# Attention in a two-layer fp32 backbone: probabilities turned by plain transposes, values multiplied four query blocks at a time, inverse sums applied to the result

## What is computed

```python
s_win = jnp.einsum("bqjhd,bqrjchd->bhqjrc", qb, kw) + bias[None]
s_ctx = jnp.einsum("bqjhd,bnhd->bhqjn", qb, k_ctx)
logits = jnp.concatenate([s_win.reshape(...), s_ctx], axis=-1)
p = jax.nn.softmax(logits.astype(jnp.float32), axis=-1)
out = (jnp.einsum("bhqjrc,bqrjchd->bqjhd", p_win, vw)
       + jnp.einsum("bhqjn,bnhd->bqjhd", p_ctx, v_ctx))
```

## Time and profile before

| what | value |
|---|---|
| median of three runs | 2733.43 us (2731.22 to 2735.35) |
| span of the profiled execution, first to last instruction | 2731.1 us |
| time of that execution beside its span | not listed; the span is 2.3 us under the median |
| PE busy | 2582.5 us (95%), 12026 instructions |
| PE weight loads busy | 2108.8 us (77%) |
| DVE busy | 1236.3 us (45%) |
| POOL busy | 1070.7 us (39%) |
| ACT busy | 583.4 us (21%) |
| attention: first logits to first matmul of the output projection | 417.06 to 730.16 us |

### The profile page before, as it was taken

The page is one execution under the profiler, slowest core; times in us unless marked ns, Lnnn a source line. Parts: engine busy times, 40 slices in busy tenths (PEclk is TensorE's granted clock), DMA queues, the critical chain, the costliest instruction groups (busy, mean ns, idle before and its releaser), DMA issues.

```text
span 2731.1 us, 33304 instructions
## 1 busy us (share of the span) xinstructions
PE 2582.5 (95%) x12026; PEld 2108.8 (77%) x12026; DVE 1236.3 (45%) x1748; ACT 583.4 (21%) x1070; POOL 1070.7 (39%) x529
## 2 busy tenths in 40 slices
PE   7898897989998999999999989999899999999999
PEld 3677776878886888888888868888678888888887
DVE  5666647867457433333222363433752222222224
ACT  4533334545323000000000140000320001000002
POOL 2223337654366333333433313343434444333330
PEclk9999998999999999999999999999899999999999
DMA  8333344321223333331111101111111111111111
GB/s 284 113 118 116 108 137 105 74 43 48 81 82 117 107 108 108 108 108 62 46 47 53 47 16 47 47 54 47 39 47 47 46 47 53 46 54 46 46 31 62
DMA packets 213972, 204.15 MB, mean 75 GB/s; under 512 B 31371, under 2 KB 184694, under 8 KB 213366
## 3 DMA queue, kind: packets, MB, share of 16 engines
q1 hardware_dynamic: 207398, 184.05, 22.6%
q10 hardware_dynamic: 5904, 16.78, 1.6%
q0 software_dynamic: 576, 2.10, 0.2%
HBM read 185.07 MB, written 19.81 MB: 75 GB/s over the span
## 4 chain that ended last, share of the span: by engine, by line
PE 77%; DVE 11%; issue 6%; ACT 3%; DMA 2%; POOL 1%; DVEq 0%; SPq 0%; ACTq 0%; POOLq 0%
PE bank L652 23%; PE bank L653 23%; PE bank L654 23%; PE bank L825 3%; PE bank L770 2%; DMA mod_in_p<-in_mod_w 1%; DVE h L1275 1%; DVE x_conv L1395 1%; PE bank L733 1%; DVE sumsq L1233 1%; DVE pt_lo L1477 1%; PE bank L815 1%; DVE scaled L1253 1%; PE bank L816 1%; DVE lru_i L1411 1%
## 5 line engine op out<-in xcount | busy, mean ns | idle before, releaser
L525 POOL TENSOR_TENSOR w_hi<-raw,ones 128x1024 fp32r<-128x1024 f32 x200 | 392.0, 1960 | 1360.3 <-PE bank L654 1115.2
L652 PE MATMUL bank<-act_hi,w_hi 128*128 128x512 f32 x2176 | 855.3, 393 | 15.3 <-DVE act_lo L1259 8.6
L653 PE MATMUL bank<-act_hi,w_lo 128*128 128x512 f32 x2176 | 851.6, 391 | 0.0
L654 PE MATMUL bank<-act_lo,w_hi 128*128 128x512 f32 x2176 | 851.0, 391 | 0.0
L528 POOL TENSOR_TENSOR w_lo<-raw,w_hi 128x1024 fp32r<-128x1024 f32 x200 | 508.9, 2544 | 15.7
L652 PEld LDWEIGHTS bank<-act_hi,w_hi 128*128 128x128 f32 x2176 | 411.4, 189 | 107.4 <-DVE act_lo L1259 11.5
L654 PEld LDWEIGHTS bank<-act_lo,w_hi 128*128 128x128 f32 x2176 | 411.3, 189 | 86.3
L653 PEld LDWEIGHTS bank<-act_hi,w_lo 128*128 128x128 f32 x2176 | 411.5, 189 | 85.0
L1275 DVE SCALAR_TENSOR_TENSOR h<-bank,mods,h 128x512 f32<-128x512 f32 x432 | 320.6, 748 | 246.6 <-PE bank L654 244.4
L1511 DVE TENSOR_TENSOR hid_f<-silu_g,bank 128x512 f32<-128x512 f32 x88 | 60.6, 688 | 707.4 <-PE bank L654 706.1
L652 PE MATMUL bank<-hid_hi,w_hi 128*128 128x512 f32 x704 | 280.7, 399 | 15.2 <-DVE h L1275 15.1
(11 more groups left out here) (183 smaller groups left out, 2713.6 us busy)
## 6 DMA issues: line engine op xcount, KB each, us to landing
raw<-in_ffn_w_gu SPq DMA_DIRECT2D x88, 512.0 KB, 3.8
mod_in_f<-in_mod_w SPq DMA_DIRECT2D x48, 512.0 KB, 4.6
raw<-in_ffn_w_down SPq DMA_DIRECT2D x44, 512.0 KB, 3.5
mod_in_p<-in_mod_w SPq DMA_DIRECT2D x32, 512.0 KB, 4.3
raw<-in_o_w_in SPq DMA_DIRECT2D x24, 512.0 KB, 3.8
raw<-in_e_w_in SPq DMA_DIRECT2D x20, 512.0 KB, 5.4
mod_ring<-in_mod_w SPq DMA_DIRECT2D x16, 512.0 KB, 4.5
raw<-in_e_w_out SPq DMA_DIRECT2D x16, 512.0 KB, 4.2
```

Of the source, the lines that this page charges most:

```text
L525: nc.gpsimd.tensor_tensor(w_hi, raw[:, parity, :], ones[:, 0:1].to_broadcast([P, UNIT]), ALU.mult).then_inc(s_hi, 1)
L652: pe.matmul(dst, w_hi, x_hi, start=first, stop=False)
L653: pe.matmul(dst, w_lo, x_hi, start=False, stop=False)
L654: return pe.matmul(dst, w_hi, x_lo, start=False, stop=last)
```

## The change

The probabilities stay as the exponentials are, without a division. A step's context logits are copied into `probs` next to the window's by a DVE operation of the same kind as the window's, which yields their minimum; one ACT instruction then takes all exponentials with one sum. Wide steps take 640 window columns (five full tiles) in place of 576. PE turns the tiles with plain transposes against the identity. Values are multiplied for four steps at once, each value tile by all the steps that read it, 128 to 512 columns, all rows; the products of a block are dealt over three of the following four steps (three spans each, the last has two). For a block, DVE takes four reciprocals in one instruction, PE spreads them over the partitions by four matmuls against the identity, ACT copies the spread rows to SBUF, and DVE multiplies the result with them into `y_f`; ACT and DVE split that.

The order changes with it: PE turns step j, then spreads or multiplies values of the block before, then scores step j+3. The loop of two rounds is written out. Most buffers of the stage move: two heads' raw keys and queries go to buffers of their own, the recurrent results are all reloaded at once and split by POOL after all heads, and the first three output weights are split once the block before the last is multiplied. The output projection begins with the recurrent half of its inputs and waits for the attention half only then. h is reloaded once all scores are done.

```diff
@@ PE @@
-                pe.wait_ge(s_exp, STEPS * i + s + 1)
+                if s >= 2:
+                    pe.wait_ge(s_min, s - 1)
...
-                    return pe.matmul(dst, probs[s % 4][:, src], inv_diag[:, s % 4, :], start=True, stop=True)
...
+            def turn_probs(s):
+
+                p, w, of = probs[s % 3], width(s), slots(s % TT)
+                pe.wait_ge(s_exp, s + 1)
+                if s:
+                    pe.wait_ge(s_ptl, 2 * s - 1)
+                for n in range(4):
+                    mm = pe.transpose(bank[:, 4, n * P:(n + 1) * P], p[:, of[n] * P:(of[n] + 1) * P], ident[:])
...
+                if 4 in of:
+                    pe.transpose(bank[:, 5, 0:P], p[:, of[4] * P:(of[4] + 1) * P], ident[:])
+                for x in range(CT):
+                    mm = pe.transpose(bank[:, 5, (x + 1) * P:(x + 2) * P], p[:, w + x * P:w + (x + 1) * P], ident[:])
...
+            def inverse_spread(g):
+
+                pe.wait_ge(s_inv, g + 1)
+                if g:
+                    pe.wait_ge(s_invr, g)
+                for j in range(4):
+                    mm = pe.matmul(bank[:, 7, j * P:(j + 1) * P], inv[:, 4 * g + j:4 * g + j + 1].to_broadcast([P, P]), ident[:],
+                                   start=True, stop=True)
...
+            def values(g, part):
+
+
+                slot, buf, every = g // 4 % 2, g % 2, spans(g % 2)
+                if part == 0:
+                    pe.wait_ge(s_ptl, 8 * g + 8)
...
+                    if g:
+                        pe.wait_ge(s_yf, g)
+                for n in range(3 * part, min(3 * part + 3, len(every))):
+                    to, tile, i0, i1 = every[n]
+                    mm = product(bank[:, 6, i0 * P:i1 * P], (v_hi[:, slot, tile, :], v_lo[:, slot, tile, :]),
+                                 pt_hi[buf][:, i0:i1, to, :], pt_lo[buf][:, i0:i1, to, :], n == 0, n == len(every) - 1)
...
+            for j in range(-3, STEPS + 4):
+                if 0 <= j < STEPS:
+                    turn_probs(j)
+                if j >= 4 and j % 4 == 0:
+                    inverse_spread(j // 4 - 1)
+                if j >= 5 and j % 4:
+                    values((j - 5) // 4, (j - 5) % 4)
+                if j + 3 < STEPS:
+                    scores(j + 3)
@@ ACT @@
+                nc.scalar.activation(probs[s % 3][:, 0:w], probs[s % 3][:, 0:w], ACT.Exp, bias=low_all[:, s:s + 1], scale=-1.0,
+                                     accum_out=sums[:, s:s + 1]).then_inc(s_exp, 1)
...
+                nc.scalar.copy(inv_rows[rows, :], bank[rows, 7, :]).then_inc(s_invr, 1)
...
+                nc.scalar.copy(act_hi[block_of(g)], y_f[block_of(g)]).then_inc(s_yh, 1)
@@ DVE @@
+                steps.run(V.tensor_tensor_reduce(out=probs[s % 3][:, w:w + CTX], in0=bank_f[:, o + w:o + w + CTX],
+                                                 in1=zero[:, 0:1].to_broadcast([P, CTX]), scale=1.0, scalar=FAR, op0=ALU.add,
+                                                 op1=ALU.min, accum_out=low_ctx[:, s:s + 1]))
+                V.tensor_tensor_reduce(out=probs[s % 3][:, 0:w], in0=bank_f[:, o:o + w], in1=bias_t[:, hd % 2, at0:at0 + w],
+                                       scale=1.0, scalar=low_ctx[:, s:s + 1], op0=ALU.add, op1=ALU.min,
+                                       accum_out=low_all[:, s:s + 1]).then_inc(s_min, 1)
...
+            def inverse_sums(g):
+                dve.wait_ge(s_exp, 4 * g + 4)
+                V.reciprocal(inv[:, 4 * g:4 * g + 4], sums[:, 4 * g:4 * g + 4]).then_inc(s_inv, 1)
...
+            def y_scaled(g):
+                rows, pair, sl = block_of(g)
+                dve.wait_ge(s_pv, g + 1)
+                dve.wait_ge(s_invr, g + 1)
+                V.tensor_tensor(y_f[rows, pair, sl], bank[rows, 6, :], inv_rows[rows, :], ALU.mult).then_inc(s_yf, 1)
...
+            for j in range(-2, STEPS + 7):
+                if j + 2 < STEPS:
+                    logits(j + 2)
+                if j >= 8 and j % 4 == 0:
+                    y_scaled(j // 4 - 2)
+                if 0 <= j < STEPS:
+                    turned_low(j)
+                if j >= 3 and j % 4 == 3 and j < STEPS:
+                    inverse_sums(j // 4)
+                if j >= 10 and j % 4 == 2:
+                    y_low(j // 4 - 2)
@@ POOL @@
+                steps.run(nc.gpsimd.tensor_copy(mid[:, 0:9, :], edge[:, 2:11, :]))
+                steps.run(nc.gpsimd.memset(mid[:, 9, :], FAR))
...
+            pool.wait_ge(s_rin, 16 * LT)
+            for j in range(LT):
+                split_lru(j)
+            for j in range(2 * FT):
+                free = (s_pv, BLOCKS - 1) if j < 3 else (s_yf, BLOCKS) if j == 3 else used_o(j - 4)
+                split(U_O + j, j % 4, j % 2, free)
@@ SP @@
+            for j in range(LT):
+                sp.dma_start(r_f[:, j, :], r_spill[j]).then_inc(s_rin, 16)
...
+            sp.wait_ge(s_sc, STEPS)
             sp.dma_start(h[:, 0:3, :], h_spill[:, 0:3, :]).then_inc(s_reload[0], 16)
```

More of the change, by code:

```diff
@@ L286, in backbone, with slots, spans, block_of @@
         V_ORDER = list(range(TT, V_TILES)) + list(range(TT))
[L287 to L294, removed]
+        STEPS = TT * HEADS
+        BLOCKS = STEPS // 4
+        LABELS = 6
+        def slots(b):
+            first, count = window(b)[0] // P, 4 + window(b)[1]
+            labels = [c if b < 4 else TT - 1 - c for c in range(first, first + count)]
+            return {0 if n == LABELS - 1 else n: r for r, n in enumerate(labels)}
+        def spans(half):
+            out_ = []
+            for n in (1, 2, 3, 0, 4, 5):
+                c = n if half == 0 else TT - 1 - n
+                at_ = [i for i in range(4) for f, wide in (window(4 * half + i),) if f // P <= c < f // P + 4 + wide]
+                out_.append((0 if n == LABELS - 1 else n, c, at_[0], at_[-1] + 1))
+            return out_[:3] + [(5 + x, TT + x, 0, 4) for x in range(CT)] + out_[3:]
+        def block_of(g):
+            hd, half = divmod(g, 2)
+            return slice(64 * (hd % 2), 64 * (hd % 2) + 64), hd // 2, slice(half * HALF, (half + 1) * HALF)
+        def width(s):
+            return MID if window(s % TT)[1] else HALF
         GROUPS = ((0, 0), (1, 0), (0, 1), (1, 1), (0, 2), (2, 0), (2, 1), (2, 2), (3, 0), (3, 1))
@@ L582, in split_head @@
                 slot = head % 2
+                k_from, q_from = (k_raw0, q_raw0) if head < 2 else (k_raw, q_raw)
                 pool.wait_ge(s_hraw, 64 * (head + 1))
@@ L799, in _, with scores @@
             pe.wait_ge(s_vev, V_TILES)
-            def scores(i, s):
+            def scores(s):
                 hd, b = divmod(s, TT)
@@ L879, in project_out @@
                 pe.wait_ge(s_split, U_O + half * FT + m + 1)
-                return columns(dst, (m + 2) % 4, act_hi, act_lo, slice(half * HALF, (half + 1) * HALF))
+                w_hi, w_lo = w_slot(slot)
+                sl = slice(half * HALF, (half + 1) * HALF)
+                for n in range(FT):
+                    k = (n + LT) % FT
+                    if half * FT + m == 0 and k == 0:
+                        pe.wait_ge(s_yl, BLOCKS)
+                    w = (w_hi[:, k * P:(k + 1) * P], w_lo[:, k * P:(k + 1) * P])
+                    mm = product(dst, w, act_hi[:, k, sl], act_lo[:, k, sl], n == 0, n == FT - 1)
@@ L882, in _ @@
+                return mm
             out_groups(0, project_out, N_F0)
@@ L1489, in _ @@
[L1489 to L1500 removed]
+                    dve.wait_ge(s_bias, hd + 1)
```

282 lines of the change are left out of this document (101 added, 181 removed).

## The result

The changed kernel takes 2635.82 us at the median of four runs (2631.84 to 2639.73) where the kernel before takes 2732.32: a ratio of 0.9647, 95% interval 0.9634 to 0.9661, 96.5 us less. 2640 was forecast. The profiled execution is the slowest of the four (2639.73, span 2637.9).

The account below looks back on a forecast made before the run. The prediction took TensorE first, then DVE, to bound the stage from first logits to output projection. 56 steps at 3.3 us plus opening and end gain 93.0: 2731.1 - 93.0 + 2.3 = 2640.4 us; range 2617 to 2678.

Parts of the forecast that it names:

- TensorE's sum after: TensorE's work per four-step block in the changed attention stage: 11.98 us, or 3.0 a step.
- The sum before: TensorE's work per four-step block in the kernel before: 15.5 us, or 3.88 a step.
- the new minimum: DVE's context minimum over 256 columns, each step: about 0.47 us, 0.75 with the wait behind it.
- the low half: DVE's low half of the result, once a block: 0.62 us, stretched up to 2.7 at worst while POOL works.
- The pace: Time per step of the changed attention stage: 3.3 us, from 13.2 a block; 3.15 to 3.5 had 60%.
- the walk: Block laid out step by step across TensorE and DVE: 12.7 us, 13.2 if the low half is stretched.
- Opening and end: Head 1's bias ready at 443.7, step 8 turned about 446.4; last spread and values done at 637.2 us.
- The handshake at 3.7: Rival: waits between engines cost as much as before, 3.7 us a step, gain 70.6, kernel 2662.8 us; 19%.
- The slower clock: Rival: transposes drop TensorE's clock to 1.2 GHz for the stage, 5.3 us a step, kernel 2757 us; 4%.
- The transpose no cheaper: Rival: a transpose costs as much as the product it replaces, 4.0 us a step, kernel 2679 us; 2%.
- TensorE alone: Rival: TensorE alone sets the stage's pace at 2.98 us a step, gain 111, kernel 2622 us; 14%.
- a visible cause: DVE's diagonal of inverse sums, 289 ns median, up to 2719, named for mean 4.66 against 4.1 us a step.

Follow-up runs that it names:

- b_nodiag: Kernel before without add, reciprocal and diagonal on DVE; turns still plain products, with the identity, normalisation left out: 2693.52 us, ratio 0.9870.
- c_even_psum: Changed kernel with scores issued before values, head 1's keys split earlier, values dealt evenly over four steps, scaled result in PSUM: 2618.14 us, ratio 0.9589.
- scores first: Changed kernel with TensorE issuing each step's scores for three steps on before the spread and value products: 2624.25 us, ratio 0.9609.
- c_first_head1: Changed kernel with scores issued before value products and head 1's keys and queries split before the first values: 2618.73 us, ratio 0.9588.
- a_pairs: Changed kernel with value products for two query blocks at once (256 columns at most) instead of four: 2631.25 us, ratio 0.9627.
- b_transposes: Kernel before with each probability tile turned by one transpose; diagonal still built and waited for, normalisation left out of the output: 2714.41 us, ratio 0.9938.
- b_both: Kernel before with transposes for turns and no add, reciprocal or diagonal on DVE, normalisation left out: 2661.55 us, ratio 0.9746.

## Why the prediction was right

**TensorE's sum after**, 3.0 a step: 3.03 in the version that keeps PE busy throughout, 2.8 by the shortest times above. The term that was too large is the transposes, forecast at 0.123 and measured at 0.097 in the step shown, 2.5 us a block for 3.2. Values, 4.61 a block: 633.57 to 638.26, 4.69. The sum before, 3.88, was close, 2% too low: b_nodiag runs its steady steps with PE busy throughout (two heads, 16 steps, from the starts of L1456):

```profile
576.78:640.39 63.61, 63.36 (x470) 57.43 (x470) 38.91 (x92) 37.00 (x109) 33.17 (x25) 1.00 0.23 58
```

That is 3.98 a step.

**DVE**: the new minimum takes 418 ns at the median against 0.47 us, and with the wait behind it 0.47 (497.57 to 498.04) against 0.75, so DVE's step was forecast 0.3 too long: its shortest steps are 2.13 narrow and 2.40 wide, for 2.43 and 2.71. Against that, the low half is stretched to 3241 ns, beyond the 2.7 us that the upper bound of 3.4 a step allowed for it; three of the sixteen took over 3.2. ACT is busy 61 of 90 us, 2.2 a step for 2.5.

**The pace**: 3.28 for 3.3. The steady four steps of the walk, forecast at 12.7, are 2.40, 2.79, 3.69 and 3.66 (12.5) or 2.13, 3.05, 3.90 and 3.59 (12.7), from the starts of L1489 after 505 us; the steps with three 512-column spans and with two are the long ones, as the walk had them. Stretched low halves bring the mean to 13.1. The order of events was foreseen; that the sum came out so exactly is in part luck, since its terms were off in both directions: turns 0.1 a step and DVE's minimum 0.3 a step too long, but the time from a matmul's start to its reader 0.31 us (a turn to ACT) and 0.43 to 0.46 (the last score product, 256 columns, to DVE) for the 0.2 to 0.25 of the walk.

**Opening and end.** The wait for head 1's bias on DVE and PE, in the timeline:

```profile
444.68 0.42 DVE L1486 CUSTOM_DVE_ANT_0 probs<-bank,zero 128x256 f32<-128x256 f32 x1 [10.57 <-POOL bias_t L599]
...
446.65 1.09 PE L848 MATMUL bank<-ident,probs 128*128 128x128 f32 x4 [5.64 <-DVE pt_lo L1502]
...
450.96 1.05 PE L848 MATMUL bank<-ident,probs 128*128 128x128 f32 x4
```

PE's clock after it, in windows, and the end of the stage in the timelines of POOL and PE:

```profile
446.60:450.00 3.40, 3.35 (x14) 3.28 (x15) 2.44 (x8) 2.16 (x6) 3.32 (x3) 0.50 0.56 101
453.00:460.00 7.00, 7.00 (x45) 6.22 (x44) 5.30 (x15) 5.34 (x11) 6.76 (x4) 1.00 0.00 1
```

```profile
633.82 2.40 POOL L552 TENSOR_TENSOR w_lo<-raw,w_hi 128x1024 fp32r<-128x1024 f32 x1
...
632.65 1.16 PE L864 MATMUL bank<-ident,inv 128*128 128x128 f32 x8 [0.96 <-DVE inv L1495]
633.57 0.48 PE L673 MATMUL bank<-pt_hi,v_hi 128*128 128x512 f32 x1
...
638.26 0.45 PE L673 MATMUL bank<-act_hi,w_hi 128*128 128x512 f32 x1
```

Head 1's bias was ready at 444.55, 443.7 was forecast (this is one execution: in the four other kernels with POOL's old order it was ready between 439.9 and 445.2); but step 8 was turned at 450.96 and not at 446.4. Two things were missing in that term. On DVE the logits of step 8 wait for the bias, and the subtraction of step 6 is queued behind them, so PE stood still for 5.64 us and then had step 7 to turn as well (446.65). And PE came out of this wait at a granted clock of 0.50, the lower level, back at 1.00 by 453: from turn 7 to turn 8 it took 4.31 us, where the same groups at their shortest take 2.2, so about 2 us of the 4.6 are the clock. Most of the 4.6 us was made up: the 56 steps from turn 8 to the last spread (632.65) took 181.7 us for 184.8, and the last spread and values 5.6 instead of 6. The projection began at 638.26 for 637.2: 91.9 us earlier than in the earlier trace rows, 93.0 forecast. The opening was too short in the forecast and the pace too slow, and that the two nearly cancel is luck. The first output weight was split at 636.2, in time, as forecast.

**The rivals.** The handshake at 3.7: 3.28, of which 0.25 lie over the 3.03 of c_even_psum, and scores first takes away 0.2 of these. The slower clock: 0.98 to 0.99 with a fifth of the time in transposes (2.5 of 13.1 us a block). The Trainium skill (TensorE: Matmul & The Clock Gate, Part 4: PE-mode transpose) says that transposes don't count as busy time for the full clock; the transposes that run alone at the start of the kernel before, 477 ns at most and 272 at least, disagree. The stage itself can't tell, as four fifths of its time is other work. The transpose no cheaper: undoing it costs 20.8 us, not the 39 between 2640 and 2679; TensorE had slack, 83 of 90 us busy. TensorE alone, 2622: not in this kernel, but c_first_head1 reaches it with another order.

**What was wrong behind the right number.** The prediction gave the mean of 4.66 us "a visible cause", the stretched diagonal, and said that most of the overhead over TensorE's sum was that. Most of it was: the mean lies 0.7 a step over the 3.98 that b_nodiag shows for TensorE's sum, and b_nodiag gained 36 us, 0.56 a step. But 27.95 us of the 293.5 are one gap where the loop turns. The other 62 intervals have a mean of 4.28; the gap, less one such step and less what the five short steps of the refill give back (12.8 us for 21.4), is 15 us, 0.24 a step. (The two shares overlap: in b_nodiag the gap is 22.4 us.) The diff wrote the loop out and the prediction had no term for it. The forecast held because the pace after was laid out step by step and not carried over from before.

**The gain, added up**: 68 (turns and diagonal together) and 12 (full rows) are shown by runs, though of kernels that leave the normalisation out. The rest of the 96.5, some 14 to 16 us, is a balance: the drain (about 13, worked out) and an earlier end of the stage, less the spread and scaling that put the normalisation back. Scores released by the minimum and the single exponential have no run of their own. No gain of the value products for four blocks at once was found (a_pairs).

## What to carry over

Where two engines bound a stage one behind the other, cut both: here 15 and 36 us alone were 68 together. Look at the starts of one line, not at its mean, before you name a pace: a single gap where a loop turns was a third of the overhead here (0.24 of 0.7 us a step), and the short steps of the refill behind it make the other steps look faster than they are. And in an in-order queue, put what another engine waits for ahead of what nobody waits for yet: the same instructions ran 0.2 us a step faster.

## What the runs showed of the hardware

The same DVE operation (64 x 512, 16 times) took 671 to 697 ns with one input in PSUM. With both in SBUF it took 673 to 690 ns in the six cases in which POOL ran nothing meanwhile, and 752 to 3241 in the ten in which it did. The Trainium skill (SBUF — State Buffer, Who interferes with whom) says that a DVE instruction with two SBUF inputs contends with a GpSimd instruction that reads SBUF, and one with at most one, outside the two-port modes, does not; the trace agrees. The number of inputs alone doesn't settle it: the diagonal of the kernel before reads one tile and a column of scalars, from SBUF into SBUF, and took 285 to 290 ns whenever POOL ran nothing and up to 2719 beside it.

PE's granted clock in the window from 450 to 540 us was 0.85 with PE busy for 67 us (b_transposes) and 1.00 with 79 (b_both). Right after the opening's wait of 5.64 us it was 0.50. How much of its gain b_transposes lost to the clock was not measured by itself.
